# Head norms of a hybrid decoder step: samples' queries by themselves, one reciprocal for the rest, key gathers behind the query weights, row factors from row sums

## The reference, cut to what matters

```
h = rms_norm(x, g_norm1) * (1.0 + sc1) + sh1        # sc1, sh1 from silu(c) @ w_ada
proj = h @ w_in                                     # q|k|v|glu_a|glu_b|gate_a|gate_c
q = rms_norm(q.reshape(B, S, N_HEADS, HEAD_DIM), g_q)
k = rms_norm(k.reshape(B, S, N_HEADS, HEAD_DIM), g_k)
```

## Time and profile before

| | us |
|---|---|
| median of 3 runs | 606.52 (602.89 to 610.44) |
| the profiled execution | 604.84 |
| its span, first to last instruction | 603.1 |
| TensorE busy | 530.6 |
| VectorE busy | 420.9 |
| ScalarE busy | 290.1 |
| GpSimd busy | 166.2 |

### The profile page before, as it was taken

How to read it: one execution, slowest core, us unless ns; L and a number is a source line. 1 busy time by engine, 2 the same in 40 slices (tenths; PEclk the granted TensorE clock), 3 DMA queues, 4 the chain that set the end, 5 groups by cost and what they waited for, 6 DMA issues and landing times.

```text
span 603.1 us, 10415 instructions
## 1 busy us (share of the span) xinstructions
PE 530.6 (88%) x4172; PEld 451.5 (75%) x4172; DVE 420.9 (70%) x614; ACT 290.1 (48%) x517; POOL 166.2 (28%) x225
## 2 busy tenths in 40 slices
PE   4784797788889898898979889979999999999997
PEld 3563587675657556475737878879999999999996
DVE  1383679998898989999865685467565665645441
ACT  2042452467776686775464452355434444333341
POOL 8245424358586686863010000000000000000000
PEclk9987997989798897988979999999999999999999
DMA  8998419758999999999864998976645644656611
GB/s 326 354 406 320 140 48 372 240 186 328 383 369 386 369 411 382 394 368 379 343 275 152 391 387 287 368 237 207 213 140 187 223 150 111 169 162 166 164 37 37
DMA packets 82127, 159.31 MB, mean 264 GB/s; under 512 B 2572, under 2 KB 61112, under 8 KB 76951
## 3 DMA queue, kind: packets, MB, share of 16 engines
q1 hardware_dynamic: 76256, 89.27, 44.3%
q0 software_dynamic: 5120, 67.71, 28.4%
q10 hardware_dynamic: 703, 1.67, 0.7%
HBM read 156.39 MB, written 2.72 MB: 264 GB/s over the span
## 4 chain that ended last, share of the span: by engine, by line
PE 53%; DVE 24%; DMA 9%; issue 6%; ACT 6%; SPq 1%; POOL 1%; ACTq 1%; DVEq 0%; POOLq 0%
PE acc L1485 12%; PE acc L1486 12%; PE acc L1487 11%; DVE prod L1003 7%; PE acc L1374 5%; DVE sall L1010 5%; DMA wring<-in_w_in 3%; DMA wring<-in_w_ada 3%; DMA wring<-in_w_ffn_in 2%; DVE oT L978 2%; ACT L603 2%; PE acc L1322 2%; PE chain L1509 1%; PE acc L1313 1%; DVE wlo L1073 1%
## 5 line engine op out<-in xcount | busy, mean ns | idle before, releaser
L1073 DVE TENSOR_TENSOR wlo<-wring,whi 128x1024 fp32r<-128x1024 f32 (+2 forms) x84 | 92.0, 1097 | 71.7 <-ACT whi L603 70.8
L603 ACT ACTIVATE whi<-wring 128x1024 fp32r<-128x1024 f32 (+2 forms) x84 | 80.1, 958 | 83.2 <-PE acc L1487 77.6
L1485 PE MATMUL acc<-xlo,whi 128*128 128x264 f32 x384 | 110.1, 287 | 3.5 <-DVE wlo L1073 1.3
L1486 PE MATMUL acc<-xhi,wlo 128*128 128x264 f32 x384 | 108.8, 283 | 0.0
L1487 PE MATMUL acc<-xhi,whi 128*128 128x264 f32 x384 | 108.7, 283 | 0.0
L1374 PE MATMUL acc<-hT,wring 128*128 128x264 f32 x336 | 98.7, 445 | 2.6 <-DMA wring<-in_w_in 2.2
L560 POOL TENSOR_TENSOR cvT<-cvT,cprod 128x256 f32<-128x256 f32 x120 | 87.6, 730 | 47.9 <-ACT cprod L603 33.1
L1374 PEld LDWEIGHTS acc<-hT,wring 128*128 128x128 f32 x336 | 70.2, 220 | 20.7 <-issue 4.6
L1485 PEld LDWEIGHTS acc<-xlo,whi 128*128 128x128 f32 x384 | 72.3, 188 | 5.8 <-issue 3.1
L1010 DVE TENSOR_REDUCE sall<-prod 128x32 f32<-128x2048 f32 x32 | 73.0, 2280 | 0.4
L1486 PEld LDWEIGHTS acc<-xhi,wlo 128*128 128x128 f32 x384 | 72.4, 188 | 0.1
(11 more groups left out here) (289 smaller groups left out, 943.2 us busy)
## 6 DMA issues: line engine op xcount, KB each, us to landing
wring<-in_w_ffn_in SPq DMA_DIRECT2D x22, 1024.0 KB, 7.7
wring<-in_w_ada SPq DMA_DIRECT2D x20, 1024.0 KB, 13.1
wring<-in_w_in SPq DMA_DIRECT2D x12, 1024.0 KB, 9.7
wring<-in_w_ffn_out SPq DMA_DIRECT2D x16, 704.0 KB, 5.6
more<-in_w_out SPq DMA_DIRECT2D x4, 1024.0 KB, 13.7
more<-in_w_ada SPq DMA_DIRECT2D x4, 1024.0 KB, 12.4
wring<-in_w_in SPq DMA_DIRECT2D x6, 512.0 KB, 15.1
wring<-in_w_in SPq DMA_DIRECT2D x4, 768.0 KB, 14.0
```

Of the source, the lines that this page charges most:

```text
L603: return nc.scalar.activation(out, in_, f, **kw)
L1073: v.tensor_tensor(wlo[:, place, 0:n, :], w, whi[:, place, 0:n, :].bitcast(F32), ALU.subtract)\
L1485: mm(bank[:, 0:R], whi[:, place, k - k0, :], lo[:, k, :], start=k == 0, stop=False)
L1486: mm(bank[:, 0:R], wlo[:, place, k - k0, :], hi[:, k, :], start=False, stop=False)
```

## The change

- Row factors: ScalarE squares x by rows with a running sum (three activations), takes three roots; VectorE inverts 128 x 3 numbers, spreads them on diagonals, and three matmuls with ones lay them on all partitions (`spread_factor`), from where the scaling reads them.
- The state transposes and their products stand before modulation slots 1 to 3, in two double tiles instead of four; VectorE copies two of the four modulation banks; ScalarE scales three of h's eight tiles.
- The 32 sample columns of q get a square, sum, root, reciprocal and product of their own (`qsq`, `qroot`, `qsn`), as soon as q3 is there.
- The squares of the eight tiles of q and k are summed by matmuls with a selector of 16 columns (`wsel`) into one tile of 16 head rows x 264; one root, one reciprocal; matmuls with `headrows` spread them (`spread_norm`), and `head_norm` multiplies with factors in PSUM (six instructions, q's two by two).
- GpSimd does all subtractions but q2's. The first gather stands behind q1's, the second behind k0's, the third behind v0's, the fourth behind v2's, v(0,0) behind v3's.
- a0 and b0 are projected before the row transposes; the own scores move into pass 0; sample 1's first product stands before it.

```diff
--- before.py
+++ after.py
-            "k3", "sqk2", "v0", "sqk3"]
-         + [f"v{t}" for t in range(1, 4)] + ["ks", "vn0", "vn1", "vs", "a0", "b0", "so", "kn0", "kn1", "a1", "b1"])
+FILLS = (["c"] + [f"x{t}" for t in range(8)] + ["vec", "st0", "st1", "adt"]
+         + [f"{x}{t}" for x in "qkv" for t in range(4)] + ["a0", "b0", "vn0", "vn1", "vs", "ks", "kn0", "kn1", "so", "a1", "b1"])
 for _b in range(B - 1):
     FILLS.append(f"g{FIRST_GATE[_b]}")
     if _b == B - 2:
@@ -108,9 +106,10 @@
 SPLITS = ([("q", t, f"q{t}") for t in range(1, 4)] + [(x, t, f"{x}{t}") for x in "kv" for t in range(4)]
           + [("glu", 0, "a0"), ("glu", 2, "b0"), ("glu", 1, "a1"), ("glu", 3, "b1")])
...
 ON_DVE = tuple(name for _, _, name in SPLITS if name not in ON_POOL)
 PRE_RING = 4
+H_BY_DVE = 5
 
...
@@ -572,17 +588,21 @@
                 pool.wait_ge(phi_ready, SPLIT[name] + 1)
                 g.tensor_tensor(low, w, high.bitcast(F32), ALU.subtract).then_inc(rest_by_pool, 1)
 
-            for name in ON_POOL[:7]:
+            for name in ON_POOL:
                 rest(name)
-            pool.wait_ge(acc_full, NUMBER[LAST_FILL["k"]] + 1)
-            gather_k(2)
-            gather_v(0, 0)
-            for name in ("v2", "v3"):
-                rest(name)
-            gather_k(3)
-            for name in ("a0", "a1", "b1"):
-                rest(name)
-            gather_k(4)
+                if name == "q1":
+                    gather_k(0)
+                if name == "k0":
+                    gather_k(1)
+                if name == "v0":
+                    pool.wait_ge(acc_full, NUMBER[LAST_FILL["k"]] + 1)
+                    gather_k(2)
+                if name == "v2":
+                    gather_k(3)
+                if name == "v3":
+                    gather_v(0, 0)
+                if name == "b1":
+                    gather_k(4)
...
+            for t in range(3):
+                rows = slice(0, P if t < 2 else B)
+                func(squares[t][rows, :], xn[rows, t, :], ACT.Square, accum_out=rowsq[rows, t:t + 1]).then_inc(row_sq, 1)
+            act.wait_ge(row_sq, 3)
+            func(rowfac, rowsq, ACT.Sqrt, scale=1.0 / D, bias=eps[:, :]).then_inc(row_root, 1)
 
...
+            for t in range(H_BY_DVE, KD):
+                func(hT[:, t, 0:S], hT[:, t, 0:S], ACT.Identity, scale=gs[:, t, 0:1], bias=modT[:, t, 0:1])\
+                    .then_inc(h_by_act, 1)
...
             high("q2")
+            raw("q", 0)
             high("q3")
-            raw("q", 0)
+            square("q", 0)
+            raw("q", 1)
             high("k0")
...
+            raw("q", 2)
+            high("k1")
+            raw("q", 3)
+            wait_freed(act, "q2")
+            wait_freed(act, "q3")
+            func(qsq, qT[:, :, S:R], ACT.Square).then_inc(qsq_ready, 1)
+            act.wait_ge(qsq_summed, 1)
+            func(qroot, chain[:, 0:32].rearrange("p (t b) -> p t b", t=4), ACT.Sqrt, scale=1.0 / DH, bias=eps[:, :])\
+                .then_inc(qroot_ready, 1)
+            square("q", 2)
+            square("q", 3)
             raw("k", 0)
+            high("k2")
+            act.wait_ge(qs_turned, 1)
+            act.wait_ge(consts, 3)
+            func(qsplit[32:32 + B, :], psS[32:32 + B, :], ACT.Copy).then_inc(qs_ready, 1)
...
+            raw("k", 1)
+            high("k3")
+            square("k", 1)
+            raw("k", 2)
             high("v0")
-            bank = when_full(act, "qs")
-            act.wait_ge(consts, 3)
-            func(qsplit[32:32 + B, :], bank[32:32 + B, :], ACT.Copy).then_inc(qs_ready, 1)
...
+            square("k", 2)
+            raw("k", 3)
+            square("k", 3)
+            high("v1")
+            raw("v", 0)
+            act.wait_ge(sq_used, 8)
+            func(headsums, small[0:2 * H, 0:R], ACT.Sqrt, scale=1.0 / DH, bias=eps[0:2 * H, :]).then_inc(head_root, 1)
+            high("v2")
+            raw("v", 1)
+            high("v3")
+            raw("v", 2)
+            high("a0")
+            high("b0")
+            raw("v", 3)
...
+            dve.wait_ge(row_root, 1)
+            step(v.reciprocal(rowfac, rowfac))
+            for t in range(3):
+                n = P if t < 2 else B
+                v.tensor_scalar(rowdiag[0:n, P * t:P * t + n], ident[0:n, 0:n], rowfac[0:n, t:t + 1], None, ALU.mult)\
+                    .then_inc(row_diag, 1)
             wait_freed(dve, "x7")
...
+            dve.wait_ge(row_spread, 1)
+            step(v.tensor_tensor(hT[:, :, :], xT[:, :, :], spread_factor.unsqueeze(1).to_broadcast([P, KD, R]), ALU.mult))
...
-            def head_norm(name, t):
-
-                wait_freed(dve, f"sq{name}{t}")
-                root = roots[t]
-                step(v.reciprocal(root, root))
-                tile = qkvT[:, "qk".index(name) * 4 + t, :]
-                g = V_GQ if name == "q" else V_GK
-                v.scalar_tensor_tensor(tile, tile, vec[:, g:g + 1], root, ALU.mult, ALU.mult)\
-                    .then_inc(q_ready if name == "q" else k_ready, 1)
...
+            dve.wait_ge(qroot_ready, 1)
+            step(v.reciprocal(qroot, qroot))
+            v.scalar_tensor_tensor(qsn, qT[:, :, S:R], vec[:, V_GQ:V_GQ + 1], qroot, ALU.mult, ALU.mult).then_inc(qsn_ready, 1)
+            dve.wait_ge(qs_ready, 1)
+            v.tensor_tensor(qsplit[32:32 + B, :], psS[32:32 + B, :], qsplit[32:32 + B, :].bitcast(F32),
+                            ALU.subtract).then_inc(qlo_ready, 1)
+
+            def head_norm(n):
+
+                bank = normbank[n]
+                dve.wait_ge(norm_spread, n + 1)
+                if n < 2:
+                    tile, g = qT[:, 2 * n:2 * n + 2, 0:S], V_GQ
+                    factor = bank[:, :].rearrange("p (t r) -> p t r", t=2)
+                else:
+                    tile, g, factor = kT[:, n - 2, :], V_GK, bank[:, 0:R]
+                v.scalar_tensor_tensor(tile, tile, vec[:, g:g + 1], factor, ALU.mult, ALU.mult).then_inc(norm_read, 1)
...
-            for half in range(STEPS):
-                score(0, half)
-                if half < 2:
-                    for t in range(2 * half, 2 * half + 2):
-                        head_norm("k", t)
-                        dve.wait_ge(k_ready, t + 1)
-                if half % 2 == 0:
-                    rest(("v1", "b0")[half // 2])
+            score(0, 0)
+            score(0, 1)
+            score(0, 2)
+            dve.wait_ge(head_root, 1)
+            v.reciprocal(headsums, headsums).then_inc(head_inv, 1)
+            score(0, 3)
+            for n in range(4):
+                head_norm(n)
+            dve.wait_ge(norm_read, 4)
             v.memset(chain[:, :], 0.0).then_inc(chain_zero, 1)
...
+            multiply(1, 0)
+            for n in range(4, 6):
+                head_norm(n)
...
+                if b >= 1:
+                    multiply_next(0)
                 dve.wait_ge(gs_ready, b + 1)
                 v.tensor_copy(gsT[:, :], sums_).then_inc(gst_ready, 1)
+                if b == 0:
+                    own_scores()
+                    dve.wait_ge(consts, 3)
+                    gated_glu(0)
+                    dve.wait_ge(u_ready, 1)
...
+            pe.wait_ge(row_diag, 3)
+            for t in range(3):
+                n = P if t < 2 else B
+                ins = mm(spread_factor[:, P * t:P * t + n], ones[0:n, :], rowdiag[0:n, P * t:P * t + n], start=True, stop=True)
...
+            for n in range(1, 4):
                 first_modulation(n)
...
+            def head_sums(n):
+
+                pe.wait_ge(sq_ready, n + 1)
+                mm(small[0:2 * H, 0:R], wsel[:, 14 - 2 * n:30 - 2 * n], tmp2[:, n % 4, :], start=n == 0, stop=n == 7)\
+                    .then_inc(sq_used, 1)
...
+                for e in range(2 if n < 2 else 1):
+                    first, width = (4 * n + 2 * e, S) if n < 2 else (2 * n + 4, R)
+                    ins = mm(bank[:, S * e:S * e + width], headrows[:, DH * first:DH * first + P],
+                             headsums[:, 0:width], start=True, stop=True)
+                ins.then_inc(norm_spread, 1)
...
             w = slot_ready("q")
-            tile("q0", w, 0, hT, ready=h_ready)
-            for t in range(1, 4):
-                split(f"q{t}")
-                head_sums("q", t - 1)
-                if t < 3:
-                    state_turned(2 * t - 2)
-                    state_turned(2 * t - 1)
-            split("k0", k1=6)
-            head_sums("q", 3)
+            tile("q0", w, 0, hT)
+            split("q1")
+            split("q2")
+            head_sums(0)
+            split("q3")
+            head_sums(1)
+            split("k0", k1=2)
+            pe.wait_ge(qsq_ready, 1)
+            mm(chain[:, 0:32], halves[:, :], qsq.rearrange("p t b -> p (t b)"), start=True, stop=True).then_inc(qsq_summed, 1)
+            split("k0", k0=2, k1=6)
+            pe.wait_ge(qsn_ready, 1)
+            for t in range(4):
```

(48 more changed lines are left out.)

223 lines of the change are left out of this document (112 added, 111 removed).

## The result

The changed kernel took **589.35 us** (median of 4 runs, 588.94 to 593.89) beside 607.38 us of the kernel before (4 runs, 602.89 to 610.44): a ratio of 0.973, 95% interval 0.968 to 0.977. 586 was forecast, with a range from 579 to 597. The profiled execution took 588.94 (span 587.2), against 604.84 of the profiled one before: 15.9 us less.

The account below looks back on a forecast made before the run. Bounds before the passes: transfers to 48 us, key weights to 54, the query chain to 79, VectorE to 118. 13.6 + 4.1 + 3.1 - 0.9 = 19.9 us gained; 585 from the profiled run, 586.6 from the median; predicted 586, range 579 to 597.

Parts of the forecast that it names:

- Stage 1: From the start until q3 is projected: q3 ends at 52.5 instead of 66.12, gain 13.6 us.
- Stage 2: From q3 to the first product of sample 0: 9.0 us instead of 13.1, gain 4.1 us.
- Stage 3: From sample 0's first product to the pass's sum: 36.6 us instead of 39.7, gain 3.1 us.
- the ring of weight tiles: In stage 3, raw copy, rounding and GpSimd's subtraction become the bound instead of VectorE, at 4.0 us per tile.
- Stage 4: Inside the pass, to the end of sample 1's first sum: 4.6 us after the pass's sum instead of 3.7, loss 0.9.
- VectorE would idle some 8 us before the sum: Sign in the profile after: VectorE idle some 8 us before it copies the pass's sum at 98.
- TensorE's work without a pause over 3 us from 44 to 90: Sign in the profile after: TensorE shows no pause over 3 us between 44 and 90 us.
- each pass is bound by VectorE: Passes after the start stay as they were, VectorE-bound, busy 24.19 of 26 us, with the same transfers per pass.
- Late key weights: Rival: transfers keep the key weights back to 54, k0 starts 4.7 us later, 591; with the slower ring counted in, 0.20.
- Given back in the passes: Rival: passes are bound by transfers, not VectorE, and wait for gathers; a third of the gain stays, 598; chance 0.11.
- Ring slower or faster: Rivals in stage 3: slower ring 591, sharing 0.20 with late key weights; ring at 3.2 per tile, 581, chance 0.07.
- Slower than before: Rival: gathers behind GpSimd's subtractions come so late that sample 0's products wait for each, 615; chance 0.03.

Follow-up runs that it names:

- the kernel with full rows added: Changed kernel with another product of the same columns over all 128 rows before each of the eight norm-spreading matmuls: 600.48 us, ratio 0.989.
- the row work put back: Changed kernel with the removed 128x8x264 product and 128x264 reciprocal put back on VectorE ahead of the scaling, results unused: 590.02 us, ratio 0.973.
- the first experiment: Changed kernel with its first two key gathers back ahead of all subtractions: 595.52 us, ratio 0.982 to the kernel before.
- the one with VectorE's wait filled: Changed kernel with sample 1's first sum and second product moved out of pass 0 into VectorE's wait for the pass's sum: 589.83 us, ratio 0.971.
- the one-pass version: Changed kernel with its small head-norm products in fp32r, the factors split into a rounded part and a rest: 583.52 us, ratio 0.964.

## Why the prediction was right, and what it mis-sized

**Stage 1** (13.6 forecast; q3's raw copy from 66.12 to 54.03, 12.1). The mechanism is as told: the gathers' place and ScalarE's order, worth 7.2 and 2.9 us at this copy when put alone into the kernel before. Most of the missing 1.5 us are in the first tile. I had taken 0.7 us off it because VectorE scales five tiles instead of eight, and VectorE did that in 1.70 us instead of 4.90; but TensorE's tile took 5.51 us, 5.42 before, at a granted clock of 0.50 from 40 to 42 and 0.77 from 42 to 44 us, and q1 was copied at 47.46, 1.2 us later than forecast. The steps of q1 followed it without a wait. TensorE of the changed kernel:

```profile
38.98 5.51 PE L1452 MATMUL acc<-hT,wring 128*128 128x264 f32 x16 [2.35 <-DMA wring<-in_w_in]
44.13 0.48 PE L1465 MATMUL acc<-hsplit,phi 128*128 128x264 f32 x1
```

In the kernel with the doubled spreadings, the same up to here, the clock was 1.00 and the tile took 3.83 us. It won nothing either, for then q1 waited for VectorE's subtractions for h (L1021):

```profile
39.45 3.83 PE L1452 MATMUL acc<-hT,wring 128*128 128x264 f32 x16 [2.33 <-DMA wring<-in_w_in]
...
43.76 0.36 PE L1465 MATMUL acc<-hsplit,phi 128*128 128x264 f32 x1 [0.48 <-DVE hsplit L1021]
```

These took 4.88 us in the changed kernel, where GpSimd's first subtraction stands beside them, and 2.83 before, where they stand alone (7.07 in the kernel with full rows added, whose q1 waited 1.69 us more for them). VectorE of the kernel before, and then GpSimd after:

```profile
43.03 2.83 DVE L954 TENSOR_TENSOR hsplit<-hT,hsplit 128x264 fp32r<-128x264 f32 x8
```

```profile
40.48 2.36 POOL L589 TENSOR_TENSOR wrest<-wring,phi 128x1024 fp32r<-128x1024 f32 x1 [18.36 <-ACT phi L623]
```

I had looked for this collision only from 61.5 us on. The Trainium skill's rule on instructions with two SBUF inputs ("SBUF — State Buffer", Who interferes with whom) agrees with these rows. In the changed kernel's own profile it delays no step of TensorE; it is what stands next once the first tile is faster.

**Stage 2** (4.1 forecast, 3.7 measured: 9.4 us from q3 to the first product instead of 9.0). Right, step by step: k0's copy at 60.08, the low part from 62.06, the product at 63.47. The key weights, which k0 needed early, were there by 47.75, and ScalarE did not wait. By the Trainium skill's equal turns of queues ("DMA: Bandwidth & Descriptors", Queues, rings and completion order) I had estimated that beside two gathers they would land near 50; in the experiment with two gathers beside them they landed at 54.05, again later than by equal turns.

**Stage 3** (3.1 forecast; 39.7 us became 40.4, a loss of 0.7). This is the term that was mis-sized, and its step was "the bound becomes the ring of weight tiles". The pace of 4.0 us per tile came true (k1 at 66.93, v2 at 86.77: five tiles in 19.8 us), but by luck, for the ring did not set it: the steps of five tiles are 14.6 us, the wait for GpSimd in them is 0.44, and nearly all the rest is six sums and a query's broadcast on TensorE. TensorE was the bound, so each product of the norms lengthens the stretch. I had put 0.6 us for the two spreadings of norms; there are eight, and they took 2.8 and 1.1 us. I took a product over 16 rows for cheap; it costs what 128 rows cost (0.5 us and 0.53). v3 was copied at 93.33 instead of 87.0 and the sum came at 103.87 instead of 98.1, 5.8 us late: 2.0 were there at the first product, 1.8 came until k1 (its last steps took 0.22 us each instead of 0.12, at a granted clock of 0.50 from 64 to 66 us, behind the eight small products for the samples' rows and a wait of 1.76 us for their low part; where the clock stayed at 1.00, with the row work put back, the way from the first product to k1 was 1.97 us instead of 3.46), 2.6 until v3 (the first six spreadings), and what stands behind it was 0.6 shorter than forecast.

**Stage 4** (a loss of 0.9 forecast): 4.8 us from the pass's sum to the end of sample 1's first sum instead of 3.7, a loss of 1.1. Right.

**The sum**: 12.1 + 3.7 - 0.7 - 1.1 = 14.0 us, and the passes gave back nothing; 1.9 came in them, most of it in the first two. VectorE waited less for ScalarE there (7.9 us in 183 instead of 10.3), but no run shows that this is the cause. That is 15.9 us in the profiled runs against 19.9 forecast. The forecast is nearer than this by luck: the unforeseen gain in the passes hides a third of the ledger's miss of 5.9 us, and the two medians lie 18.0 us apart, the profiled run of the kernel before being 2.5 us below its median. That VectorE would idle some 8 us before the sum was right as a length (8.33), but both its ends came six us late, at 96.0 and 104.3 instead of 90 and 98; the fourth sum ended at 86.4 instead of 82. TensorE's work without a pause over 3 us from 44 to 90 was right. That each pass is bound by VectorE is refuted for pass 0, which did not get shorter when 4.6 us of VectorE's work left it.

**The rivals.** Late key weights: refuted here; the first experiment prices them at 3.1 us at the first product and 4.1 at the end of the profiled runs, where 4.7 was forecast. Given back in the passes: refuted; no wait for a gather is in the trace. Ring slower or faster: not the bound. Slower than before: refuted.

**What stays open.** What exactly the clock answers to. It fell behind the small fp32 products that spread the norms in eight profiles, doubled or not, in blocks or apart, over 16 rows or half of them over 128, for some 3 to 23 us, and not in three (the changed kernel's first profile, the one with VectorE's wait filled, the one-pass version). But it fell at nearly the same place in the kernel before, which spreads no norms: 0.50 from 94 to 100 us, after TensorE had stood idle from 91 to 94. In the passes it falls at times too, in the one-pass version from 102 to 105 us, so it isn't the norms' alone. How often the one-pass version keeps the clock up to the pass's sum, its one profile does not tell, but its six runs are all below the fastest run of the changed kernel. Open too is what the samples' own chain and the joint head norms are worth each by itself: no run takes either out.

## What to carry to other kernels

When an engine is relieved, list the remaining work of every other engine in that stretch, product by product with its measured duration, before naming the next bound: the change's own new small matmuls were the term here. A transfer that is needed first should not share the transfer engines with ones that are needed later, and a copy that frees a bank should stand ahead of any instruction that waits for a transfer. Time freed on an engine that only fills a chain, as VectorE in pass 0, buys nothing.

## What the runs showed of the hardware

- A float32 product of 16 contraction rows and 264 columns took about 0.5 us, as one of 128 rows (0.53); in fp32r four of 256 columns took 0.64 to 0.74. A reciprocal of 16 x 264 took 1.79 us, one of 128 x 264 took 1.80.
- In eight of eleven profiles the granted clock fell from 1.00 to 0.50 behind or among such products while TensorE was busy without a pause. From v2's raw copy to the copy of the pass's sum took 17.5 us at a clock of 1.00 (the changed kernel), 22.2 with it low from 93 to 103 us (the changed kernel again), and 29.0 with the doubled products, some 3.9 of them the doubling, and the clock low from 93 to 109.
- The first tile of q, in float32, took 3.83 us at a granted clock of 1.00, and 5.25 to 6.49 in profiles where it was 0.50 for part or all of the tile (5.51 in the changed kernel, 6.49 in its second profile).
- VectorE's eight subtractions with both inputs in SBUF took 2.83 us alone, 4.88 beside one subtraction of GpSimd's, and 7.07 in the one profile where a second one began beside them.
- Two transfers of keys beside the weights delay these by over 6 us: 54.05 against 47.75 or less.
